# Expert weights applied before the rows are stored, and gathers that add into the residual rows

## What is computed

```
top_v, top_i = lax.top_k(logits, TOP_K)          # TOP_K = 2
top_p = jax.nn.softmax(top_v, axis=-1)
combine = jnp.sum(jax.nn.one_hot(top_i, N_EXPERTS) * top_p[..., None], axis=1)
for e in range(N_EXPERTS):
    out = out + combine[:, e:e + 1] * swiglu(t, w_gate[e], w_up[e], w_down[e])
...
x = x + gt2[:, None, :] * f                      # f is out
return rmsnorm(x, final_norm_g)
```

## Time and profile before

| | |
|---|---|
| median of 3 runs | 1582.44 us (1580.9 to 1583.68) |
| the profiled execution's own time | 1587.15 us |
| its span | 1585.0 us |
| mean granted TensorE clock | 0.97 of 2.4 GHz |
| busy: PE, DVE, ACT, POOL | 1504.4 us (95%), 1161.3 us (73%), 787.4 us (50%), 64.0 us (4%) |
| chain that ended last | PE 89%, DVE 4%, DMA 3%, ACT 2% |

### The profile page before, as it was taken

The page is one execution under the profiler, slowest core; times in us unless marked ns, Lnnn a source line. Parts: engine busy times, 40 slices in busy tenths (PEclk is TensorE's granted clock), DMA queues, the critical chain, the costliest instruction groups (busy, mean ns, idle before and its releaser), DMA issues.

```text
span 1585.0 us, 22469 instructions
## 1 busy us (share of the span) xinstructions
PE 1504.4 (95%) x8952; PEld 1197.7 (76%) x8952; DVE 1161.3 (73%) x1425; ACT 787.4 (50%) x927; POOL 64.0 (4%) x49
## 2 busy tenths in 40 slices
PE   4999999989999999998999999799999999999993
PEld 2667877768888888886688768578888888888883
DVE  4779866666666665546678765579999999999994
ACT  3534246242222222224542464577777777777774
POOL 8200000000000000000000000110000000000002
PEclk8999998989999999999999999999999999999996
DMA  9453211435656664531211005299999999999975
GB/s 350 145 199 108 81 41 54 161 132 187 186 185 186 186 196 145 188 109 53 66 47 52 27 28 180 95 366 410 411 397 400 399 399 389 390 398 399 398 274 172
DMA packets 94599, 340.33 MB, mean 215 GB/s; under 512 B 10016, under 2 KB 14240, under 8 KB 91808
## 3 DMA queue, kind: packets, MB, share of 16 engines
q1 hardware_dynamic: 92192, 330.51, 57.2%
q0 software_dynamic: 2304, 8.39, 1.4%
HBM read 316.84 MB, written 22.02 MB: 214 GB/s over the span
## 4 chain that ended last, share of the span: by engine, by line
PE 89%; DVE 4%; DMA 3%; ACT 2%; issue 1%; SPq 0%; POOL 0%; POOLq 0%; ACTq 0%; DVEq 0%
PE ps L648 34%; PE ps L1219 10%; PE ps L1221 10%; PE ps L1220 10%; PE ps L951 2%; PE ps L979 2%; DMA scr<-in_ada 1%; DVE scr L1715 1%; PE ps L963 1%; PE ps L806 1%; PE ps L798 1%; PE ps L661 1%; PE ps L1061 1%; PE ps L1062 1%; PE ps L1063 1%
## 5 line engine op out<-in xcount | busy, mean ns | idle before, releaser
L1712 DVE TENSOR_TENSOR wlm<-rawm,hlo 128x2048 fp32r<-128x2048 f32 x120 | 274.8, 2290 | 21.5 <-ACT hlo L1329 20.2
L1260 ACT ACTIVATE whi<-raw 128x1024 fp32r<-128x1024 f32 (+1 forms) x112 | 123.2, 1103 | 311.0 <-PE ps L648 261.9
L1329 ACT ACTIVATE hlo<-rawm 128x2048 fp32r<-128x2048 f32 x120 | 230.1, 1919 | 70.5 <-PE ps L1221 69.2
L648 PE MATMUL ps<-hhi,whi 128*128 128x512 f32 x624 | 253.6, 406 | 1.9 <-DVE wlo L1722 1.9
L1722 DVE TENSOR_TENSOR wlo<-raw,whi 128x1024 fp32r<-128x1024 f32 (+1 forms) x112 | 144.9, 1294 | 149.1 <-ACT whi L1260 146.8
L648 PE MATMUL ps<-hlo,whi 128*128 128x512 f32 x624 | 245.1, 393 | 0.0
L648 PE MATMUL ps<-hhi,wlo 128*128 128x512 f32 x624 | 245.0, 393 | 0.0
L1220 PE MATMUL ps<-wlm,xgh 128*128 128x512 f32 x480 | 186.8, 389 | 0.0
L1712 DVE TENSOR_TENSOR wlm<-rawm,whm 128x2048 fp32r<-128x2048 f32 x60 | 137.5, 2291 | 27.5 <-ACT whm L1329 27.5
L648 PEld LDWEIGHTS ps<-hhi,whi 128*128 128x128 f32 x624 | 118.2, 189 | 38.8 <-issue 12.3
L1219 PE MATMUL ps<-hlo,xgh 128*128 128x512 f32 x360 | 141.6, 393 | 0.6 <-issue 0.6
(11 more groups left out here) (323 smaller groups left out, 2514.9 us busy)
## 6 DMA issues: line engine op xcount, KB each, us to landing
rawm<-in_wm SPq DMA_DIRECT2D x360, 512.0 KB, 8.0
raw<-in_w SPq DMA_DIRECT2D x96, 512.0 KB, 3.6
adah<-in_ada SPq DMA_DIRECT2D x56, 512.0 KB, 4.4
scr<-in_ada SPq DMA_DIRECT2D x20, 1024.0 KB, 6.5
raw<-in_w SPq DMA_DIRECT2D x16, 704.0 KB, 4.3
xs<-scr SPq DMA_DIRECT2D x15, 512.0 KB, 5.3
ys<-yb SPq DMA_DIRECT2D x15, 512.0 KB, 8.9
xg<-xs SPq DMA_DIRECT2D x14, 512.0 KB, 7.2
```

The lines of the kernel that those rows point to most:

```text
L648: ins = pe.matmul(ps[:, b, :], a, r[:, k0 + k, :], start=(start and first and k == ks[0] and n == 0), stop=(stop and last and k == ks[-1] ...
L1260: act.activation(whi[:, slot, 0:width], raw[:, slot, 0:width], ACT.Copy).then_inc(sem("hi_ready"), 1)
L1329: act.activation(hi_pair(q), raw_pair(q), ACT.Copy).then_inc(sem("him_ready"), 1)
L1712: return dve.tensor_tensor(out, a, b, op)
```

## The change

- A new tensor in HBM, `share`, holds one float for each slot. It is cleared with one more store of zeros in the first layer, and the waits on `xs_cleared` count it.
- After the softmax, DVE makes `sidx`, the place of each slot's weight in `share`, with three more small operations: place (slot & 127) * 16 + (slot >> 7). `p_ready` comes after them.
- After the scatters of the token rows, POOL scatters the weights: eight indirect DMAs of 128 elements of 4 bytes into `share`. It waits for all of them and loads `share` into `pslot` [128, 16], so that column b holds the weights of block b's slots.
- `results(b)` multiplies PSUM by `pslot[:, b]` and by the gate row in one `scalar_tensor_tensor`. For b = 0 it waits for `share_in` first.
- The eight gathers write into `htok` with an add (`compute_op=ALU.add`), so that the residual rows become the sum. For each c the gather of k = 1 waits for that of k = 0 to land. The order is c0 k0, c1 k0, c0 k1, c1 k1, c2 k0, c3 k0, c2 k1, c3 k1. Each gather of k = 0 waits for `htok_ready` of its rows. POOL's wait for the last low part (`low_done`) goes.
- `weighted` and `combine` go; `root` waits for `yg_in{c}` and reads `htok`, and `normed` reads `htok` too.

```diff
@@ POOL
-            low_done(pool, NB * NT - 1)
+            pool.wait_ge(sem("p_ready"), 1)
+            for c in range(4):
+                for k in range(2):
+                    pool.indirect_dma_start(share[:], bass.IndirectOffsetOnAxis(ap=sidx[:, k, c:c + 1], axis=0),
+                                            rt[:, 64 + 4 * k + c:65 + 4 * k + c], None).then_inc(sem("share_out"), 16)
+            pool.wait_ge(sem("share_out"), 8 * 16)
+            pool.dma_start(pslot[:], share.rearrange("(s b) o -> s (b o)", s=P)).then_inc(sem("share_in"), 16)
+
             for parity in range(2):
                 pool.wait_ge(sem(f"y_out{parity}"), 16 * ((NB + 1 - parity) // 2))
-            for c in range(4):
-                for k in range(2):
-                    pool.indirect_dma_start(yg[:, c, k, :], None, ys[:],
-                                            bass.IndirectOffsetOnAxis(ap=slots[:, k, c:c + 1], axis=0))\
-                        .then_inc(sem(f"yg_in{c}"), 16)
+            for pair in range(2):
+                for k, c in [(k, 2 * pair + q) for k in range(2) for q in range(2)]:
+                    if k:
+                        pool.wait_ge(sem(f"yg_in{c}"), 16)
+                    else:
+                        pool.wait_ge(sem("htok_ready"), (6, 7, 9, 10)[c])
+                    pool.indirect_dma_start(htok[:, c, :], None, ys[:],
+                                            bass.IndirectOffsetOnAxis(ap=slots[:, k, c:c + 1], axis=0),
+                                            compute_op=ALU.add).then_inc(sem(f"yg_in{c}"), 16)
@@ ACT
-                    def weighted(c):
-
                         act.wait_ge(sem(f"yg_in{c}"), 32)
-                        act.wait_ge(sem("p_ready"), 1)
-                        act.activation(yg[:, c, 0, :], yg[:, c, 0, :], ACT.Copy, scale=rt[:, 64 + c:65 + c])\
-                            .then_inc(sem("y_weighted"), 1)
-
-                    def root(c):
-
-                        act.wait_ge(sem("z_ready"), c + 1)
-                        mark(act.activation(sqj, yg[:, c, 0, :], ACT.Square, accum_out=rt[:, 80 + c:81 + c]), "act_step")
+                        mark(act.activation(sqj, htok[:, c, :], ACT.Square, accum_out=rt[:, 80 + c:81 + c]), "act_step")
@@ DVE
-                        tt(yb[:, b % 2, :], ps[:, 6:8, :].rearrange("p b n -> p (b n)"), frow[:, 0, :])\
+                        if b == 0:
+                            dve.wait_ge(sem("share_in"), 16)
+                        stt(yb[:, b % 2, :], ps[:, 6:8, :].rearrange("p b n -> p (b n)"), pslot[:, b:b + 1], frow[:, 0, :],
+                            ALU.mult, ALU.mult)\
...
-                    def combine(c):
-
-                        y = yg[:, c, 0, :]
-                        dve.wait_ge(sem("y_weighted"), c + 1)
-                        dve.wait_ge(sem("htok_ready"), (6, 7, 9, 10)[c])
-                        link(stt(y, yg[:, c, 1, :], rt[:, 68 + c:69 + c], y))
-                        tt(y, y, htok[:, c, :], ALU.add).then_inc(sem("z_ready"), 1)
...
-                        stt(yg[:, c, 1, :], yg[:, c, 0, :], rt[:, 88 + c:89 + c], frow[:, 1, :], ALU.mult, ALU.mult)\
+                        stt(yg[:, c, 1, :], htok[:, c, :], rt[:, 88 + c:89 + c], frow[:, 1, :], ALU.mult, ALU.mult)\
```

More of the change, by code:

```diff
@@ L251, in trunk @@
             slots = sb("slots", [2, 4], I32, stack=room)
+            sidx = sb("sidx", [2, 4], I32, stack=room)
+            pslot = sb("pslot", [16], stack=room)
         xs = nc.dram_tensor("xs", (NB * P, D), F32, kind="Internal").ap()
         ys = nc.dram_tensor("ys", (NB * P, D), F32, kind="Internal").ap()
+        share = nc.dram_tensor("share", (16 * P, 1), F32, kind="Internal").ap()
         def rawm_tile(g):
@@ L458, in _ @@
                     sp.dma_start(xs[t * P:(t + 1) * P, :], ZERO).then_inc(sem("xs_cleared"), 16)
+                    if t == 0:
+                        sp.dma_start(share.rearrange("(p n) o -> p (n o)", p=P), ZERO[:, 0:16])\
+                            .then_inc(sem("xs_cleared"), 16)
                 if t == 3:
@@ L561, in _ @@
                 turn(pool.tensor_scalar(ang[:, n, :], ang[:, n, :], -float(np.float32(3.1415925)), None, ALU.max))
-            pool.wait_ge(sem("xs_cleared"), 16 * NB)
+            pool.wait_ge(sem("xs_cleared"), 16 * (NB + 1))
             pool.wait_ge(sem("slots_ready"), 1)
@@ L1652, in _, with root @@
                                 tokens(b + 1)
-                    def weighted(c):
+                    def root(c):
                         act.wait_ge(sem(f"yg_in{c}"), 32)
-                        act.wait_ge(sem("p_ready"), 1)
-                        act.activation(yg[:, c, 0, :], yg[:, c, 0, :], ACT.Copy, scale=rt[:, 64 + c:65 + c])\
-                            .then_inc(sem("y_weighted"), 1)
-                    def root(c):
-                        act.wait_ge(sem("z_ready"), c + 1)
-                        mark(act.activation(sqj, yg[:, c, 0, :], ACT.Square, accum_out=rt[:, 80 + c:81 + c]), "act_step")
+                        mark(act.activation(sqj, htok[:, c, :], ACT.Square, accum_out=rt[:, 80 + c:81 + c]), "act_step")
                         act.activation(rt[:, 84 + c:85 + c], rt[:, 80 + c:81 + c], ACT.Sqrt, scale=1.0 / D, bias=C("eps"))\
@@ L1679, in _ @@
                     turned_rows(9, 2, htok[:, 2, :])
-                    weighted(0)
                     turned_rows(10, 4, htok[:, 3, :])
-                    weighted(1)
                     root(0)
-                    weighted(2)
                     root(1)
                     turned_back(0)
-                    weighted(3)
                     root(2)
@@ L2121, in _ @@
                 if layer == 0:
-                    dve.wait_ge(sem("xs_cleared"), 16 * NB)
+                    dve.wait_ge(sem("xs_cleared"), 16 * (NB + 1))
                     for i in range(FC):
@@ L2242, in _ @@
                     link(dve.reciprocal(rt[:, 64:68], four(3)))
-                    tt(rt[:, 68:72], four(2), rt[:, 64:68]).then_inc(sem("p_ready"), 1)
+                    link(tt(rt[:, 68:72], four(2), rt[:, 64:68]))
+                    low7 = pre[:, 0:8].bitcast(I32)
+                    high = pre[:, 8:16].bitcast(I32)
+                    flat = slots[:].rearrange("p k c -> p (k c)")
+                    link(dve.tensor_scalar(low7, flat, P - 1, 4, ALU.bitwise_and, ALU.logical_shift_left))
+                    link(dve.tensor_scalar(high, flat, 7, None, ALU.logical_shift_right))
+                    tt(sidx[:].rearrange("p k c -> p (k c)"), low7, high, ALU.bitwise_or).then_inc(sem("p_ready"), 1)
                     def results(b):
@@ L2280, in normed @@
                         link(dve.reciprocal(rt[:, 88 + c:89 + c], rt[:, 84 + c:85 + c]))
-                        stt(yg[:, c, 1, :], yg[:, c, 0, :], rt[:, 88 + c:89 + c], frow[:, 1, :], ALU.mult, ALU.mult)\
+                        stt(yg[:, c, 1, :], htok[:, c, :], rt[:, 88 + c:89 + c], frow[:, 1, :], ALU.mult, ALU.mult)\
                             .then_inc(sem("final_norm"), 1)
-                    combine(0)
-                    combine(1)
                     for c in range(4):
                         normed(c)
-                        if c + 2 < 4:
-                            combine(c + 2)
 def _chunks(a):
```

## The result

The changed kernel is slower. Its median was 1590.42 us (1588.17 to 1595.6, 7 runs) against 1582.44 (1579.92 to 1585.42, 7 runs) for the kernel before: ratio 1.0055, 95% interval 1.004 to 1.007, so 6.3 to 11.1 us more; the medians themselves differ by 8.0. A second comparison later gave 1591.51 against 1583.01, ratio 1.0054 (1.004 to 1.0068). The prediction was 1588.0, slower.

A forecast was written before the change was run, and what follows sets the result against it. PE was taken to bound the kernel, with 89% of the chain. Gather schedule 4.5, output stores 0.6, weights' scatters 0.4 and result rows 0.1 made +5.6 us on 1582.4: 1588.0 us, range 1579.5 to 1594.5.

The forecast's parts named there:

- What bounds, and where the change acts: Whole kernel: PE carries 89% of the chain, so the change can act only in block 0 and at the end.
- What the change removes: End: some 7 us from the last group's landing to its square go; ACT's and DVE's hand-written order was called late.
- The data of an adding gather: End gathers: each add takes 1.6 to 2.9 us of all DMA engines, 2.9 taken, because two operands must be read.
- The schedule of the gathers: End: landings worked out from issue, data and POOL's wake-up times; end 36.6 us after the first issue, +4.5 us.
- rival 2: End gathers: POOL takes 1.45 us more to issue each add; +10.0 us in all, 1592.4; chance 0.13.
- The wake-up before the first gather: Before the first gather: dropping POOL's `low_done` wait gains nothing, since the wait for the last store is later anyway.
- Output stores: End: the first groups' stores run among the last gathers and delay the last one by 0 to 3.6 us; +0.6 taken.
- The weights' scatters: Block 0: eight 4-byte scatters, counted as 1024 packets, delay weight loads by nothing to 1.7 us; +0.4 taken.
- Result rows as a product of three: Loop: `results` takes 1.28 for 1.22 us; 14 of 15 lie beside PE, the last is on the path; +0.1 us.
- The cover of `share_in`: Block 0: the weights land at about 1061, DVE needs them at 1072.85; the block's own matmuls hide it by 12 us.
- The sum: Whole kernel: 4.5 + 0.6 + 0.4 + 0.1 = +5.6 us, giving 1588.0 us.
- the forecast's own range: Whole kernel: 1584 to 1591 us, for adding-gather data between 2.2 and 3.5 us; chance 0.53.

The follow-up runs named there:

- e7: Kernel before, with ACT's weighting of group 3 moved ahead of its copy of group 0 out of PSUM; one execution, end stretch 31.5 us against 32.1.
- e2: Changed kernel with the k = 0 gathers of all four groups first, then the k = 1 gathers; median 1589.72 us, ratio 1.0029 to the kernel before.
- e1: Changed kernel whose eight gathers overwrite instead of adding, same order and waits; median 1583.35 us against 1583.46 for the kernel before, ratio 1.0004.
- e8: Kernel before without POOL's wait for the last low part; one execution, last result rows to first gather 4.1 us against 4.63, end stretch 31.7 us.
- e6: Changed kernel with eight more scatters of the weights, to an unread tensor, ahead of the eight that count; one execution, 1606.06 us.
- e4: Kernel before, with DVE doing residual += weight x row in one operation per gather and no weighting on ACT; median 1582.18 us, ratio 0.999.
- e3: Changed kernel with weights still applied in the rows, but plain gathers that DVE adds as each lands; median 1583.2 us, ratio 0.9994 to the kernel before.
- e9: Kernel before with both the fused DVE additions of e4 and the removed POOL wait of e8; median 1579.55 us against 1583.01, ratio 0.998.

## Why the prediction was right

**What bounds, and where the change acts**: right. Blocks 1 to 14 are 0.2 to 0.3 us longer, and all else that can be found lies after the last block.

**What the change removes**: right in size, wrong in cause. The 7 us between the last landing and the last square are gone (landing and square now meet, 1580.17 and 1580.19). I laid them to the order on ACT; `e7` shows that the order is worth 0.3 to 0.7 us. Had I summed DVE's work there (5.1 + 4.9 us and four times 1.44 for reciprocal and normed row, 15.8 in all, in the 17.2 us from 1560.86 to 1578.1) I would have seen an engine that is idle for 1.5 us in all. The forecast did not depend on the cause, since the change takes ACT's weighting and DVE's adding away together; what else could have been done about it did.

**The data of an adding gather**: right, and the step that carried the sign. I took 2.9 us, the upper end of 1.6 to 2.9; the queue showed 2.9 (changed kernel) and 2.8 (`e2`). Its two parts were each a little off and made up for each other: a plain gather is 1.5 and not 1.6, so the add brings 1.4 and not 1.3. `e1` shows that without this and the longer issue there is no loss at the end: 30.5 us where it was 32.1. With them it is 39.0. So the round trips used up most of the 7 us that the change frees, and the adds (8.5 us) made the loss. The rule of the Trainium skill (Collectives: The Full Stack, "The bandwidth ceiling: the fold count and why AG ≠ RS ≠ AR"), that a reduce has two source reads and half the rate of a copy, holds here for an indirect gather that adds: 2.9 against 1.5 us of all engines. The rate agrees; that the second read is the reason, no run shows. The prediction got 3.2 us by it only because it doubled 1.6.

**The schedule of the gathers**: right in form, each landing late, and more so with each round trip. In us after the first issue, predicted and measured (a landing is the next issue it released less 0.26, the releasing gap in the chain):

```
            c0k0  c1k0  c2k0  c3k0  c3k1  end
predicted    5.5   8.4  17.5  20.4  26.6  36.6
measured     6.3   9.1  18.1  22.2  29.3  39.0
```

The mis-sized terms: the issue is 1.54 us and not 0.95 (rival 2 in small: I priced it at 1.45 more, it was 0.6 more, and a first gather lands 6.3 us after its issue where I had 5.5); the slow gather of group 3 adds about 1 us that nothing accounts for; POOL's waking takes 0.26 us, not 0.7, and gives some back. Together 2.4 us above my 4.5.

**The wake-up before the first gather** I had at nothing. It gave 0.4 us back (4.20 against 4.63 from the last result rows), and `e8` puts that on the removed wait, a line that I had called free. It also explains the 0.74 us of the earlier trace rows, which I took for POOL's waking at every landing.

**Output stores**, +0.6: not settled. They do slow the last gathers, but the cost at the last one is 0.1 to 2.0 us by the profiles.

**The weights' scatters**, +0.4 in block 0: nothing shows, but 0.4 could not be seen beside a spread of 2 us. The upper bound of 1.7 us rested on 1024 packets; there were about 290, and they had 0.8% of the engines. The rule of the Trainium skill (DMA: Bandwidth & Descriptors, "Specifications") that less than 512 B means a read, a change and a write made no difference that a row shows.

**Result rows as a product of three**, +0.1: the last one is 0.06 us longer, as priced. That the other 14 are hidden beside PE does not hold quite: blocks 1 to 14 are 0.2 to 0.3 us longer together. No run separates this from the rest of the weights' way.

**The cover of `share_in`**: right that it holds, wrong by half in its margin. Landing at 1059.73 + 5.2 = 1064.9, need at 1070.99: 6.1 us, not 12. Six of the eight issues took 2.0 to 2.9 us where I had set 0.95. `e6` shows what lies beyond the margin: 11.7 us of PE.

**The sum**: +5.6 predicted, +8.0 in the medians, 6.3 to 11.1 by the interval. The parts read in the profile are +6.9 at the end, -0.4 ahead of it and +0.3 in the loop: 6.8. The measured 1590.42 lies inside the forecast's own range of 1584 to 1591, the second 1591.51 just above it. The sum was low by the longer issue and the slow gather; some of that was made up by luck, since POOL's waking was priced too long.

## What to carry to other kernels

A gather that adds took the DMA engines twice as long here as a plain one, and this kernel waits for its landing before it issues the next one to the same rows. By these prices it can pay only where the DMA engines are idle and the engine that would add is not; no run here shows such a case. Here it freed an engine with 1.3 us operations and paid 1.4 us for each on a busier resource, plus round trips. Before moving work off an engine, first add up its rows in the stretch. What did help was one fused operation that starts at each landing (2.5 to 2.9 us of the end stretch in `e4`) and taking a settled wait out of a queue (0.5 us in `e8`).

## What the runs showed of the hardware

- An indirect DMA of 128 rows of 4 KB takes POOL 1.53 us to issue with an add and 0.94 without, and lands after 6.2 us in a quiet queue instead of 4.2.
- Some plain issues on POOL are longer while DVE works. In the kernel `e3` the eight gathers are issued in 1.00, 0.94, 0.94, 0.94 us, and, once DVE's additions (two inputs in SBUF) have begun at 1558.48, as here:

```profile
1559.16 1.35 POOL L591 DMA_INDIRECT rawm<-ys,slots  x1 [0.31 <-issue]
1560.82 1.93 POOL L591 DMA_INDIRECT rawm<-ys,slots  x1 [0.30 <-issue]
1563.05 1.16 POOL L591 DMA_INDIRECT rawm<-ys,slots  x1 [0.30 <-issue]
1564.51 1.33 POOL L591 DMA_INDIRECT rawm<-ys,slots  x1 [0.30 <-issue]
```

  In the changed kernel, with DVE nearly always idle, all are 1.53 to 1.67. But not every issue beside DVE is longer: in `e9` the last two (1558.29 and 1559.62) took 1.02 and 0.94 us while DVE worked without a gap. The Trainium skill (SBUF — State Buffer, "Who interferes with whom") says that DVE with two SBUF inputs contends with a GpSimd instruction that reads SBUF; the rows of `e3` agree in time and those two of `e9` do not, and no run here separates the two, so it is not shown as a cause.
- A wait on POOL for something that has long happened, ahead of the wait that matters, made the first DMA after it 0.5 us later (`e8`; from the last result rows to the first gather it is 4.1 to 4.2 us in all eight profiles without it and 4.6 to 4.7 in all five with it). Why is open.
